# Two-layer encoder with expert retrieval: the one-hot operands of the routing built token by token

## What is computed

```python
q = (x @ wq).reshape(C, PEER_HEADS, 2, PEER_HALF)
s = jnp.einsum('chpk,hpnk->chpn', q, sub_keys)          # 8 heads, 2 halves, 128 keys
top_s, top_i = lax.top_k(s, K)                          # K = 16
cand = top_s[:, :, 0, :, None] + top_s[:, :, 1, None, :]
best_s, best_j = lax.top_k(cand.reshape(C, PEER_HEADS, K * K), K)
i1 = jnp.take_along_axis(top_i[:, :, 0], best_j // K, axis=-1)
i2 = jnp.take_along_axis(top_i[:, :, 1], best_j % K, axis=-1)
e = i1 * N_KEYS + i2                                    # one of 128 * 128 experts
g = jax.nn.softmax(best_s, axis=-1)
h = jax.nn.gelu(jnp.einsum('cd,chkd->chk', x, expert_u[e]))
out = jnp.einsum('chk,chkd->cd', g * h, expert_v[e])
```

## Time and profile before

| | |
|---|---|
| median of three runs | 3645.83 us |
| the profiled execution: its time | 3650.73 us |
| its span in the trace | 3648.9 us |
| TensorE matmul busy | 3368.2 us (92%), 17714 matmuls |
| VectorE busy | 2612.8 us (72%), 4731 instructions |
| ScalarE busy | 1246.3 us (34%) |
| GpSimd busy | 1351.3 us (37%) |
| mean DMA rate | 209 GB/s |

### The profile page before, as it was taken

The page is one execution under the profiler, slowest core; times in us unless marked ns, Lnnn a source line. Parts: engine busy times, 40 slices in busy tenths (PEclk is TensorE's granted clock), DMA queues, the critical chain, the costliest instruction groups (busy, mean ns, idle before and its releaser), DMA issues.

```text
span 3648.9 us, 55659 instructions
## 1 busy us (share of the span) xinstructions
PE 3368.2 (92%) x17714; PEld 2983.8 (82%) x17714; DVE 2612.8 (72%) x4731; ACT 1246.3 (34%) x2013; POOL 1351.3 (37%) x711
## 2 busy tenths in 40 slices
PE   7999998699969999999999999986998799999999
PEld 6787888588858888888877878876888688888888
DVE  4544699999867766766645547999997776766776
ACT  3433322233323333333334423222333233333332
POOL 3444344333433333333144443433434333333331
PEclk9999999899979999999999999998999899999999
DMA  3112343466688988888621123334666898888886
GB/s 117 64 52 69 113 130 107 171 226 220 257 307 314 312 300 300 303 304 309 211 96 67 52 75 110 123 111 176 223 252 243 311 320 307 303 305 300 300 303 208
DMA packets 235870, 763.87 MB, mean 209 GB/s; under 512 B 19056, under 2 KB 117488, under 8 KB 200688
## 3 DMA queue, kind: packets, MB, share of 16 engines
q1 hardware_dynamic: 198896, 494.09, 38.8%
q0 software_dynamic: 36864, 268.45, 21.4%
HBM read 684.87 MB, written 77.59 MB: 209 GB/s over the span
## 4 chain that ended last, share of the span: by engine, by line
PE 56%; DVE 17%; DVEq 14%; issue 7%; DMA 3%; POOL 1%; ACT 0%; SPq 0%; POOLq 0%; ACTq 0%
PE PS L416 18%; PE PS L418 18%; PE PS L417 18%; DVEq L1332 5%; DVEq L1336 4%; DVE EQ L1267 2%; DVE OB L1334 2%; PE PS L583 1%; DVE OE L1331 1%; DVEq L1276 1%; DVE I L1220 1%; DVE I L1227 1%; POOL RL L1407 1%; DVE OA L1330 1%; DVE SW L1221 1%
## 5 line engine op out<-in xcount | busy, mean ns | idle before, releaser
L1407 POOL TENSOR_TENSOR RL<-RAW,RH 128x1024 fp32r<-128x1024 f32 x384 | 980.4, 2561 | 1021.6 <-ACT RH L762 1021.1
L416 PE MATMUL PS<-XH,RH 128*128 128x384 f32 (+1 forms) x2720 | 990.7, 364 | 22.8 <-ACT GEL L949 22.8
L418 PE MATMUL PS<-XH,RL 128*128 128x384 f32 (+1 forms) x2720 | 962.6, 354 | 0.0
L417 PE MATMUL PS<-XL,RH 128*128 128x384 f32 (+1 forms) x2720 | 961.5, 353 | 0.0
L1441 POOL DMA_INDIRECT ROWS<-in_peer_rows,LIST x256 | 302.7, 1183 | 1138.6 <-DVE X L1315 1092.5
L416 PE MATMUL PS<-VHI,WHI 128*128 128x512 f32 x1536 | 602.3, 392 | 42.6 <-DVE WLO L1364 42.6
L418 PE MATMUL PS<-VHI,WLO 128*128 128x512 f32 x1536 | 600.8, 391 | 0.0
L417 PE MATMUL PS<-VLO,WHI 128*128 128x512 f32 x1536 | 600.7, 391 | 0.0
L416 PEld LDWEIGHTS PS<-XH,RH 128*128 128x128 f32 x2720 | 524.5, 193 | 52.1 <-POOL RL L1407 12.3
L1361 DVE TENSOR_TENSOR VLO<-VRAW,VHI 128x1024 fp32r<-128x1024 f32 x256 | 322.2, 1259 | 341.4 <-ACT VHI L957 341.4
L417 PEld LDWEIGHTS PS<-XL,RH 128*128 128x128 f32 x2720 | 522.1, 192 | 28.5
(11 more groups left out here) (227 smaller groups left out, 3487.8 us busy)
## 6 DMA issues: line engine op xcount, KB each, us to landing
RAW<-in_peer_u SPq DMA_DIRECT2D x256, 512.0 KB
VRAW<-in_peer_v SPq DMA_DIRECT2D x256, 512.0 KB, 5.9
RAW<-in_stream SPq DMA_DIRECT2D x128, 512.0 KB
route_dram<-STAGE SPq DMA_DIRECT2D x16, 3072.0 KB, 12.4
GC<-route_dram SPq DMA_DIRECT2D x64, 768.0 KB, 9.1
gelu_dram<-GS SPq DMA_DIRECT2D x128, 192.0 KB, 3.8
GB<-gelu_dram SPq DMA_DIRECT2D x32, 768.0 KB, 10.1
ROWS<-in_peer_rows,LIST POOLq DMA_INDIRECT x256, 7.8
```

The costliest lines, as they stand in the source:

```text
L416: pe.matmul(acc, sh, mh, start=first, stop=False)
L417: pe.matmul(acc, sh, ml, start=False, stop=False)
L418: return pe.matmul(acc, sl, mh, start=False, stop=last)
L1407: pool.tensor_tensor(RL[:, k % 4, :], RAW[:, k % 2, :], RH[:, k % 4, :].bitcast(F32), ALU.subtract).then_inc(S.low_part, 1)
```

## The change

Operands lie contiguously for each token, and a narrow instruction with per-partition scalars builds each token's row. The comparison with i2 and the product with a gate part are one instruction with two operations; OE is gone. [...] The loop over 8 is unrolled.

```diff
-        IOTA4 = sb("IOTA4", [P, P, 4], BF16)
+        IOTAB = sb("IOTAB", [P, P], BF16)
...
-        IT = at("IT", 48 * K, [P, 5, SD], BF16)
-        REST = at("REST", 52 * K, [P, 2, SD])
-
-        OA = at("OA", 55 * K, [P, 2, 2, P, 4], BF16)
-        OE = at("OE", 59 * K, [P, 2, P, 4], BF16)
-        OB = at("OB", 61 * K, [P, 2, 3, 2, P, 4], BF16)
+        IT = at("IT", 48 * K, [P, 5, SD])
+        PART = at("PART", 73 * K, [P, 3, SD], BF16)
+        REST = at("REST", 76 * K, [P, 2, SD])
+
+        OA = at("OA", 56 * K, [P, 2, 8, P], BF16)
+        OB = at("OB", 61 * K, [P, 2, 3, 8, P], BF16)
...
-                                    m = pe.matmul(PS[:, 4 + g % 2, t * P:(t + 1) * P], OA[:, g // 2 % 2, g % 2, :, t],
-                                                  OB[:, g // 2 % 2, p, g % 2, :, t], start=p == 0, stop=p == 2)
+                                    m = pe.matmul(PS[:, 4 + g % 2, t * P:(t + 1) * P], OA[:, g // 2 % 2, g % 2 * 4 + t, :],
+                                                  OB[:, g // 2 % 2, p, g % 2 * 4 + t, :], start=p == 0, stop=p == 2)
...
-            dve.tensor_copy(IOTA4[:], IOTA[:].unsqueeze(2).to_broadcast([P, P, 4]))
+            dve.tensor_copy(IOTAB[:], IOTA[:])
...
                 for p in range(3):
-                    dve.tensor_copy(IT[:, 2 + p, :], REST[:, p % 2, :])
+                    dve.tensor_copy(PART[:, p, :], REST[:, p % 2, :])
+                    dve.drain()
+                    dve.tensor_copy(IT[:, 2 + p, :], PART[:, p, :])
                     dve.drain()
...
-                with dve.Fori(0, 8) as i:
+                for i in range(8):
                     for u in range(6):
                         n, slot = 6 * i + u, u % 2
-
-                        def of_tokens(row):
-
-                            return IT[:, row, bass.ds(8 * n, 8)].rearrange("p (g t) -> p g t", g=2).unsqueeze(
-                                2).to_broadcast([P, 2, P, 4])
-
-                        numbers = IOTA4[:].unsqueeze(1).to_broadcast([P, 2, P, 4])
                         dve.wait_ge(S.routed, count(l, "routed", 2 * n - 2))
-                        dve.tensor_tensor(OA[:, slot], numbers, of_tokens(0), ALU.is_equal)
-                        dve.tensor_tensor(OE[:], numbers, of_tokens(1), ALU.is_equal)
-                        dve.drain()
-                        for p in range(3):
-                            m = dve.tensor_tensor(OB[:, slot, p], OE[:], of_tokens(2 + p), ALU.mult)
+                        for t in range(8):
+                            tok = slice(8 * n + t, 8 * n + t + 1)
+                            dve.tensor_scalar(OA[:, slot, t, :], IOTAB[:], IT[:, 0, tok], None, ALU.is_equal)
+                            for p in range(3):
+                                m = dve.tensor_scalar(OB[:, slot, p, t, :], IOTAB[:], IT[:, 1, tok], IT[:, 2 + p, tok],
+                                                      ALU.is_equal, ALU.mult)
                         m.then_inc(S.onehots_ready, 1)
```

## The result

The changed kernel takes 3958.59 us median (3952.26 to 3965.85, four runs) against 3645.93 us of the kernel before (3640.17 to 3653.31, four runs): 1.0857 times, 95% interval 1.083 to 1.0884, so 313 us slower. The forecast was 3845 us with a range from 3800 to 4000. Sign and range held; the size was 114 us short, and the forecast's own narrower range, 3810 to 3885, missed.

What follows compares the result with a forecast made beforehand. VectorE was taken to set the pace of the routing stages. 96 units at +2.04 us (+196 us) and preparation (+2.6 us), together +199 us on 3645.8, gave 3845 us, range 3800 to 4000, own range 3810 to 3885.

Steps and rivals of the forecast that it cites:

- What bounds the stage: In the two routing stages, VectorE sets the pace: TensorE waits 25.4 us for its one-hot products, VectorE for no engine.
- Price of a narrow instruction: VectorE's 128-element bf16 instruction: 133 ns fixed plus 33 ns of elements, 166 ns; a unit 5.40 us against 3.36.
- The second scalar: In the 24 fused instructions of a unit, a second per-partition scalar costs nothing; the other end was 59 ns each.
- that rival, at 0.24: Second scalar costs as the first: 1.42 us more a unit, +136 us, 3981 us; chance 0.24.
- Gaps: VectorE's gaps (wait, drain) in the routing stage stay at 0.4 us.
- The hold: GpSimd's subtractions still hold VectorE 2.15 us each, 2.87 us a pair of units; 138 us if it falls.
- TensorE: Contiguous operands save its one-hot matmuls up to 2.4 us a pair, or nothing; worth nothing in the time, lower clock included.
- Preparation: Before the routing stage, three more conversions of 384 elements per layer, 0.43 us each with drain: +2.6 us.
- The rival "faster": VectorE's narrow instruction costs only an immediate scalar's floor, 93 ns: a unit 3.13 us, 3627 us in all; chance 0.07.

## Why the prediction was right, and where it was short

**What bounds the stage.** Right. VectorE's waits hold nothing but gaps, TensorE's hold OB, and the two kernels with TensorE's reads exchanged show it from both sides.

**Price of a narrow instruction.** Right for the form with one scalar, 0.166 us forecast and 0.163 measured, and so is its make: 133 ns fixed (from the normalising products and the address computation; 130 measured) and 0.26 ns per element.

**The second scalar.** This is the term that was mis-sized: "I take nothing, because both scalars are known before the stream starts and could be fetched together". It costs 57 ns over the 166 of the sum; the stated other end was 59. The wide range took it in because that rival, at 0.24, lay inside it; the central value did not. This term alone is 24 x 0.057 x 96 = +131 us, more than the 114 that were missing. The rival that had it gave 3981 us, 22 from the measured time. The row argued for it: the first scalar's cost is not hidden even under 1024 elements, so nothing spoke for the second's being hidden.

**Gaps.** Forecast unchanged at 0.4; measured 0.17 and 0.28, 0.35 us a pair less, 17 us in all. The diff had the unrolled loop; that its registers cost gap time was not priced.

**The hold.** Kept at 2.87 us a pair, measured 19.61 - 16.51 = 3.10 (16.51 is 2.60 + 2 x 6.73 + 0.17 + 0.28), and 3.01 by the kernel with short subtractions. That one-input instructions are held too was read rightly from one row. The terms close: 17.05 forecast, + 2.74 for the second scalar, - 0.35 for gaps, + 0.23 for the hold are 19.67, against 19.61 measured. The last two small misses have opposite signs and nearly cancel, which is luck.

**TensorE.** The gain was bounded at 0 to 2.4 us a pair, and at full clock the upper end came true and a little more: a group went from 1.34 to 0.65 us, 2.7 us a pair. (By its rows the group before is 1.34 us, 112 ns a matmul, and not 1.3 and 108.) That it would be worth nothing in the time also came true. The clock did fall in the waits, to 0.78 granted, and cost nothing, as assumed. Those waits were 8.5 us a pair (408.5 us over 48 pairs in the trace), where 5 had been forecast, since VectorE was slower than forecast.

**Preparation.** As forecast: for each gate part a conversion to PART, which rounds it to bf16, and one back to IT, each 0.43 us with its drain.

**The rival "faster".** Its price of 93 ns was not found. By the rule of the Trainium skill ("VectorE: DVE Perf Modes", The TRN2 errata), 58 cycles and the elements, the fused form would be 94 ns, an estimate from that page; it took 223. The same section's warning that small tiles pay the fixed cost each time holds here: 32 instructions of a unit pay 130 or 190 ns each.

## What to carry to other kernels

Count the instructions of the engine that ends the waits before counting what a layout gives another engine: 32 instructions with 130 to 190 ns of fixed cost each replaced 5 of some 0.61 us each, and the fusion of two operations was paid for by a second scalar per partition. Where both engines want their own layout, look for a step that serves both; two tokens innermost did. And an engine that is held by a neighbour's instruction may be better off doing that work itself.

## What the runs showed of the hardware

A second scalar per partition costs VectorE 60 ns per instruction at 128 bf16 elements: 0.163 us from start to start with one and 0.223 with two. What the first one costs was not tested by itself. An estimate is 59 to 73 ns: the 133 ns that a form with one such scalar has beside its elements, less the 60 to 74 ns of instructions without one.

TensorE streams 128 bf16 columns at a step of 4 elements (8 bytes) in 108 to 112 ns, at a step of 2 elements or contiguous in some 56 ns, at full granted clock. At a granted clock of 0.50 the step of 4 takes no longer (1.34 us for twelve), while contiguous operands go to 1.22 us, so that there the step costs only a tenth. The step of the stationary operand made 0.03 us of difference to a group of twelve at most. The Trainium skill ("SBUF — State Buffer", Specifications) has two reads per 16-byte line as enough for full bandwidth; by it a step of 4 would have been free. For the streamed operand these runs say otherwise, and the measurement decides.

GpSimd's subtraction of 1024 fp32 columns (some 2.4 us) holds a VectorE instruction with a single bf16 tensor input, by 2.24 us in the mean, as it holds those with two inputs, by 2.15.
